# A two-layer encoder in float32 pairs: the first four projection groups ordered by chunk, their weights split at another time

## The chip, the cores and the metric

The kernel runs on one core of one Trainium2 chip. The metric is the device time of one execution in microseconds, lower is better. The core has a matrix engine (PE, with its weight loads PEld), a vector engine (DVE), an activation engine (ACT), GpSimd (POOL) and a sync engine (SP) that here only issues transfers; 16 DMA engines move the data. Each engine works through its own instructions in order and waits on semaphores for the others.

## The reference, cut to what matters

Two groups of 256 tokens (512 in all) go through two encoder layers of width 1024. The part of a layer that the change touches is its start:

```python
def encoder_layer(x, c, ...):                       # called for layer 0 and layer 1
    mod = jax.nn.silu(c) @ w_ada + b_ada            # 6 x 1024 numbers for each group of tokens
    shift1, scale1, gate1, shift2, scale2, gate2 = jnp.split(mod, 6, axis=-1)
    h = rms_norm(x, norm_attn) * (1 + scale1) + shift1
    proj = h @ w_in                                 # qa 512, ka 128, va 128, qb 512, kb 512, vb 512, gates 2048
    ...                                             # two attentions, merge, output projection
    x = x + gate1 * merged
    h2 = rms_norm(x, norm_ffn) * (1 + scale2) + shift2
    return x + gate2 * grouped_moe(h2, ...)         # 16 experts, 2 for each token
```

All of it is float32. The output is the final norm of both groups.

## The kernel before, in words

**Products of pairs.** A float32 product is made of three fast ones. An operand is split into a high part (a copy rounded to the fast type, `x_hi`, `w_hi`) and a low part (the float32 value minus the high part, `x_lo`, `w_lo`). `mm3` (L756) then issues three matmuls of 128x128 by 128x512 into the same bank: low weight by high activation (L758), high weight by low activation (L759), high by high (L760). ACT makes the high parts, DVE the low ones.

**The projection.** The activations are kept transposed, 1024 features as KC = 8 chunks of 128 partitions by 512 tokens. The input projection is cut into groups of 128 output columns (`W_GROUPS`); group n needs a 1024x128 slice of the weight, of which the high part goes into one of W_BUFS = 4 buffers (`w_hi[n % 4]`) and the low part into `w_lo`. `in_group` (L762) takes a bank, waits for the weight's low part and runs eight steps k = 0 to 7, one `mm3` for each chunk: 24 matmuls. Groups 0 to 3 are the four slices of qa, in one 2 MB weight block that lies in ring slot 1; groups 4 and 5 are ka and va. The order of the groups is the list `QKV_ORDER`. In group 0 alone, PE waits before each step for that chunk's low part (`first=True`).

**The chunks.** For chunk c, `norm_scale` (DVE, L1716) multiplies x by the reciprocal root of its mean square. `norm_split` (ACT, L1276) adds shift and scale and rounds to `x_hi`: one pair of instructions for chunks 0 and 4 (`SCALE_DVE`), a pair and a cast for the other six. `norm_low` (DVE, L1727) makes `x_lo`. PE can run step k of any group once chunk k has its low part and the group has its weights.

**The weights of the first four groups.** `high_part(layer, n)` (ACT, L1259) waits for the block to land if n is the block's first group, and casts the slice. `low_part(n)` (DVE, L1709) subtracts. Before, ACT does all four high parts ahead of the first chunk, in both layers; DVE does low part 0 ahead of the first chunk, and low parts 1 to 3 between chunks.

**What stands ahead of it.** In layer 0 the factors `rstd` are known early, and the projection waits for `mod` (from w_ada) and for the block qa. In layer 1 the outputs of the experts are added first: ACT weighs the returned rows (`weigh_first`, L1269), DVE adds the second choice and, chunk by chunk, the result to x (`combine`, L1792, and `add_gated`, L1783). ACT squares each chunk (L1253), PE sums the squares over the partitions (L844), ACT takes the root (`norm_root`, L1255), DVE the reciprocal (L1780). Only then come the chunks.

**What stands behind it.** When a qa group is complete, ACT reads its bank twice (L1361, L1364) and then makes the high part of the group four places later (`GROUP_AFTER`), DVE its low part. PE goes on to group 4 and the rest.

Of the kernel before, what the change touches and what calls it, by code (L numbers as in the profile page):

```python
# [31 lines left out]
KC = D // P  # L32
# [69 lines left out]
W_BUFS = 4  # L102
# [88 lines left out]

GROUP_AFTER = {group_key(n - W_BUFS): n for n in range(W_BUFS, QKV_GROUPS)}
# [145 lines left out]
def build_trunk(nc, t_in, y_prompt, y_sample):  # L340
# [7 lines left out]
    with ctx:  # L348
# [394 lines left out]
        def _(pe):  # L743
# [18 lines left out]
            def in_group(key, n, first=False, before=0):  # L762
# [11 lines left out]
                done(layer_use, key, ins)  # L774

            def ada_rows(layer, i):

# [69 lines left out]
            for layer in range(DEPTH):  # L847
# [20 lines left out]


                for q in QKV_ORDER:  # L870
                    last_block = None
# [28 lines left out]
                    else:  # L900
                        n = group_no("kva", ("ka", "va").index(q)) if q in ("ka", "va") else group_no(q[:2], int(q[2:]))
                        in_group(q, n, first=(n == 0))
                        b = W_GROUPS[n][0]
# [292 lines left out]
        def _(act):  # L1196
# [78 lines left out]

            def norm_split():  # L1276

                for c in range(KC):
                    act.wait_ge(S["xn_ready"], c + 1)
# [31 lines left out]
            for layer in range(DEPTH):  # L1311
# [16 lines left out]
                else:  # L1328
                    for i in range(ADA_FIRST):
                        ada_copy(i)  # L1330
                    weigh_first(layer)
                    for c in range(KC):
                        norm_square(use, "back", c, hT)
                    norm_root(use, 0)
                for n in range(W_BUFS):
                    high_part(layer, n)
                act.wait_ge(S["mod_ready"], 1)
                norm_split()

# [295 lines left out]
        def _(dve):  # L1635
# [156 lines left out]
            def combine(own, use, layer, nth):  # L1792

                for t in range(TT):
                    dve.wait_ge(S["got_weighed"], nth * TT + t + 1)
                    v.scalar_tensor_tensor(got[0][:, t, :], got[1][:, t, :], gw[:, 1, t:t + 1], got[0][:, t, :],
                                           ALU.mult, ALU.add).then_inc(S["mix_ready"], 1)
                for c in range(KC):
                    add_gated(use, ("back", c), c, 1)

            for layer in range(DEPTH):
# [32 lines left out]
                if layer:  # L1834
                    combine(own, use, layer, 0)
                    norm_rstd(own, use, 0)
                low_part(0)
                for c in range(KC + 2):
                    if c < KC:
                        norm_scale(c)  # L1840
                    if c > 1:
                        norm_low(c - 2)
                    if c in (4, 6, 8):
                        low_part(c // 2 - 1)

# [619 lines left out]
```

## Time and profile before

| | us |
|---|---|
| median of 3 runs (1573.08 to 1576.23) | 1575.25 |
| the profiled execution's own time | 1576.64 |
| its span in the trace | 1574.8 |
| PE busy | 1440.8 (91% of the span) |
| DVE busy | 1005.1 (64%) |
| ACT busy | 872.2 (55%) |
| POOL busy | 109.5 (7%) |

Busy time counts all stages together. PE is busy for most of the span, but a matmul lasts longer when the clock granted to PE is low, and that counts as busy too. The two places of the change, the start of the projection of layer 0 and of layer 1, lie at about 43 to 82 us and 793 to 850 us of the trace. What decides there is read from the timelines of the three engines, which tell for each instruction when it began and what ended the idle time before it.

### The profile page before, as it was taken

How to read it: one execution, taken by the hardware profiler on the slowest of the kernel's cores; microseconds unless marked ns; L12 is line 12 of the kernel's file. 1: busy time of each engine (PE TensorE's matmuls, PEld its weight loads, DVE VectorE, ACT ScalarE, POOL GpSimd, SP SyncE). 2: the span in 40 equal slices, each digit the busy share in tenths (PEclk: the TensorE clock that was granted, in tenths of full speed). 3: DMA queues.
4: the chain of work that ended last, by engine and by line, in shares of the span. 5: the costliest groups of instructions: out<-in, count | busy, mean ns of one | idle time of the engine just before them, and what ended most of it. 6: DMA issues, size and time to landing. Idle time of an engine off the chain costs nothing. (4 is left out here: it accounts for less than half of the span.)

```text
span 1574.8 us, 19442 instructions
## 1 busy us (share of the span) xinstructions
PE 1440.8 (91%) x6858; PEld 1095.0 (70%) x6858; DVE 1005.1 (64%) x1256; ACT 872.2 (55%) x1244; POOL 109.5 (7%) x143
## 2 busy tenths in 40 slices
PE   5799999999988999999769989899998899999996
PEld 3477667787757777777437775688875777777774
DVE  1456586334379888888363928743355888888884
ACT  4532486323256777777363318932234577777764
POOL 1000000000011111211000000000000111111100
PEclk9799999999989999999889999999998999999998
DMA  9532471223158999999762217511135599999944
GB/s 328 210 107 107 161 249 73 76 85 107 57 215 310 373 370 354 361 355 361 270 243 85 76 68 267 201 54 54 54 137 184 215 347 366 358 370 358 359 185 164
DMA packets 148368, 341.49 MB, mean 217 GB/s; under 512 B 8351, under 2 KB 10545, under 8 KB 148176
## 3 DMA queue, kind: packets, MB, share of 16 engines
q1 hardware_dynamic: 136880, 317.20, 55.4%
q0 software_dynamic: 10704, 22.57, 4.0%
q10 hardware_dynamic: 720, 0.87, 0.2%
q8 instruction: 39, 0.64, 0.2%
q14 instruction: 25, 0.20, 0.0%
HBM read 333.08 MB, written 24.12 MB: 227 GB/s over the span
## 5 line engine op out<-in xcount | busy, mean ns | idle before, releaser
L758 PE MATMUL bank<-x_hi,w_lo 128*128 128x512 f32 x608 | 246.6, 406 | 28.8 <-DVE x_lo L1736 18.7
L759 PE MATMUL bank<-x_lo,w_hi 128*128 128x512 f32 x608 | 240.0, 395 | 0.0
L760 PE MATMUL bank<-x_hi,w_hi 128*128 128x512 f32 x608 | 240.0, 395 | 0.0
L2217 DVE TENSOR_TENSOR w_lo<-ring,x_lo 128x2048 fp32r<-128x2048 f32 x92 | 210.6, 2289 | 29.5 <-ACT x_lo L1529 28.6
L1529 ACT CAST zone_r<-ring 128x2048 fp32r<-128x2048 f32 x92 | 176.0, 1913 | 28.9 <-PE bank L1106 16.4
L1529 ACT CAST x_lo<-ring 128x2048 fp32r<-128x2048 f32 x92 | 176.0, 1918 | 26.4 <-PE bank L1121 13.6
L1713 DVE TENSOR_TENSOR w_lo<-ring,w_hi 128x1024 fp32r<-128x1024 f32 x84 | 102.4, 1221 | 96.4 <-ACT w_hi L1267 95.7
L758 PEld LDWEIGHTS bank<-x_hi,w_lo 128*128 128x128 f32 x608 | 115.4, 190 | 65.9 <-issue 27.5
L1104 PE MATMUL bank<-w_lo,zone_r 128*128 128x512 f32 x384 | 156.3, 407 | 0.0
L759 PEld LDWEIGHTS bank<-x_lo,w_hi 128*128 128x128 f32 x608 | 116.1, 191 | 25.8 <-issue 2.4
L760 PEld LDWEIGHTS bank<-x_hi,w_hi 128*128 128x128 f32 x608 | 115.8, 190 | 25.0
L1106 PE MATMUL bank<-zone_r 128*128 128x512 f32 x256 | 101.3, 396 | 0.0
L1105 PE MATMUL bank<-zone_r 128*128 128x512 f32 x256 | 100.9, 394 | 0.0
L1267 ACT CAST w_hi<-ring 128x1024 fp32r<-128x1024 f32 x84 | 87.1, 1046 | 20.7 <-PE bank L760 6.1
L1105 PE MATMUL bank<-x_lo,zone_r 128*128 128x512 f32 x240 | 95.1, 396 | 0.0
L1106 PE MATMUL bank<-x_lo,zone_r 128*128 128x512 f32 x240 | 95.0, 396 | 0.0
L1464 ACT ACTIVATE zone<-bank 128x512 f32<-128x512 f32 x32 | 19.1, 598 | 136.1 <-PE bank L760 136.1
L2217 DVE TENSOR_TENSOR w_lo<-ring,zone_r 128x2048 fp32r<-128x2048 f32 x32 | 73.4, 2292 | 21.6 <-ACT zone_r L1529 21.2
L1104 PEld LDWEIGHTS bank<-w_lo,zone_r 128*128 128x128 f32 x384 | 72.4, 189 | 15.3
L2217 DVE TENSOR_TENSOR w_hi<-ring,zone_r 128x2048 fp32r<-128x2048 f32 x32 | 73.4, 2292 | 6.2 <-ACT zone_r L1529 6.0
L2032 DVE TENSOR_TENSOR zone<-bank,zone 128x512 f32<-128x512 f32 x16 | 11.1, 692 | 86.6 <-PE bank L760 86.6
L2217 DVE TENSOR_TENSOR x_hi<-ring,zone_r 128x2048 fp32r<-128x2048 f32 x28 | 63.9, 2283 | 0.0
(316 smaller groups left out, 2751.3 us busy)
## 6 DMA issues: line engine op xcount, KB each, us to landing
ring<-in_w_gate SPq DMA_DIRECT2D x32, 2048.0 KB, 13.8
ring<-in_w_up SPq DMA_DIRECT2D x32, 2048.0 KB, 15.0
ring<-in_w_down SPq DMA_DIRECT2D x32, 2048.0 KB, 9.2
ring<-in_w_ada SPq DMA_DIRECT2D x24, 2048.0 KB, 8.6
ring<-in_w_in SPq DMA_DIRECT2D x16, 2048.0 KB, 8.3
ring<-in_w_out SPq DMA_DIRECT2D x4, 2048.0 KB, 7.7
zone<-y_by_choice SPq DMA_DIRECT2D x8, 1024.0 KB, 8.1
ring<-in_w_branch_a SPq DMA_DIRECT2D x2, 2048.0 KB, 8.0
```

The costliest lines, as they stand in the source:

```text
L758: mm(out, lo, x_first, start=start, stop=False)
L759: mm(out, hi, x_second, start=False, stop=False)
L760: return mm(out, hi, x_first, start=False, stop=stop)
L1104: mm(out, xg_hi[:, par, c, :], wv[:, c, :], start=(c == 0), stop=False)
L1105: mm(out, xg_lo[:, par, c, :], hi[:, k, :], start=False, stop=False)
L1106: ins = mm(out, xg_hi[:, par, c, :], hi[:, k, :], start=False, stop=(c == KC - 1))
L1267: nc.scalar.copy(w_hi[:, n % W_BUFS, :, :], group_view(ring[SLOT[b]], b, c)).then_inc(S["w_hi_ready"], 1)
L1464: af(gates[:, n % 2, :], ps[:, :], ACT.Sigmoid).then_inc(S["gate_ready"], 1)
L1529: nc.scalar.copy(part_hi[buf], ring[EXPERT_SLOTS[par][k]][:, h * 2048:(h + 1) * 2048])\
L1713: v.tensor_tensor(group_view(w_lo[SLOT[b]], b, c), group_view(ring[SLOT[b]], b, c), w_hi[:, n % W_BUFS, :, :].bitcast(F32), ALU.subtract). ...
L2032: v.tensor_tensor(dst, ps[:, :], gates[:, n % 2, :], ALU.mult)\
L2217: v.tensor_tensor(w_low[EXPERT_SLOTS[par][k]][:, cols], ring[EXPERT_SLOTS[par][k]][:, cols], part_hi[buf].bitcast(F32), ALU.subtract)\
```

## The change

Three things change, and the arithmetic stays the same: the same matmuls, casts and subtractions on the same operands.

- PE runs groups 0 to 3 by a list of (group, step) pairs, `FIRST_GROUPS`, and no longer one group after another. It takes groups 0 and 1 for chunks 0 to 3, then groups 2 and 3 for chunks 0 to 3, then all four for chunk 4, then each group's last three steps. Each group has its own bank throughout.
- In layer 0, ACT no longer makes the four high parts first, but one behind chunk 1, 1, 2 and 3 (`SPLIT_ORDER`). DVE's order is `LOW_ORDER` (s: `norm_scale`, x: `norm_low`, w: `low_part`).
- In layer 1, ACT makes the four high parts behind `weigh_first` and ahead of the squares; DVE makes low part 0 ahead of `add_gated`, and low parts 1 to 3 behind it, ahead of the reciprocal.

```diff
+FIRST_GROUPS = ([(n, k) for n in (0, 1) for k in (0, 1)] + [(n, k) for k in (2, 3) for n in (0, 1)]
+                + [(n, k) for n in (2, 3) for k in range(4)] + [(n, 4) for n in range(W_BUFS)]
+                + [(n, k) for n in range(W_BUFS) for k in range(5, KC)])
+SPLIT_ORDER = ("x0", "x1", "w0", "w1", "x2", "w2", "x3", "w3", "x4", "x5", "x6", "x7")
+LOW_ORDER = ("s0", "s1", "x0", "s2", "x1", "w0", "s3", "w1", "x2", "w2", "s4", "x3", "w3", "s5", "x4", "s6", "x5", "s7",
+             "x6", "x7")
...
+            def first_groups():
+                for n, k in FIRST_GROUPS:
+                    b, c = W_GROUPS[n]
+                    if k == 0:
+                        take(layer_use, f"{b}{c}")
+                        pe.wait_ge(S["w_lo_ready"], n + 1)
+                    if n % 2 == 0:
+                        pe.wait_ge(S["x_lo_ready"], k + 1)
+                    ps = bank[layer_use[f"{b}{c}"][0]]
+                    ins = mm3(ps[:, :], w_hi[:, n, k, :], group_view(w_lo[SLOT[b]], b, c)[:, k, :], x_hi[:, k, :],
+                              x_lo[:, k, :], k == 0, k == KC - 1)
+                    if k == KC - 1:
+                        done(layer_use, f"{b}{c}", ins)
...
+                first_groups()
                 for q in QKV_ORDER:
...
-                        in_group(q, n, first=(n == 0))
+                        if n >= W_BUFS:
+                            in_group(q, n)
...
-            def norm_split():
-                for c in range(KC):
+            def norm_split(layer):
+                for what in SPLIT_ORDER:
+                    c = int(what[1:])
+                    if what[0] == "w":
+                        if layer == 0:
+                            high_part(layer, c)
+                        continue
                     act.wait_ge(S["xn_ready"], c + 1)
...
                     weigh_first(layer)
+                    for n in range(W_BUFS):
+                        high_part(layer, n)
                     for c in range(KC):
                         norm_square(use, "back", c, hT)
                     norm_root(use, 0)
-                for n in range(W_BUFS):
-                    high_part(layer, n)
                 act.wait_ge(S["mod_ready"], 1)
-                norm_split()
+                norm_split(layer)
...
+                low_part(0)
                 for c in range(KC):
                     add_gated(use, ("back", c), c, 1)
+                for n in range(1, W_BUFS):
+                    low_part(n)
...
-                low_part(0)
-                for c in range(KC + 2):
-                    if c < KC:
+                for what in LOW_ORDER:
+                    c = int(what[1:])
+                    if what[0] == "s":
                         norm_scale(c)
-                    if c > 1:
-                        norm_low(c - 2)
-                    if c in (4, 6, 8):
-                        low_part(c // 2 - 1)
+                    elif what[0] == "x":
+                        norm_low(c)
+                    elif layer == 0:
+                        low_part(c)
```

PE, start of the projection in layer 0, in the order of issue with bank and buffer numbers. Before, group 0 fills bank 0 and each of its steps waits for a chunk:

```order
L758 MATMUL bank0<-x_hi,w_lo1 128x512 [waits x_lo_ready,w_lo_ready,free0]
L759 MATMUL bank0<-x_lo,w_hi 128x512
L760 MATMUL bank0<-x_hi,w_hi 128x512
L758 MATMUL bank0<-x_hi,w_lo1 128x512 [waits x_lo_ready]
...
L758 MATMUL bank1<-x_hi,w_lo1 128x512 [waits w_lo_ready,free1]
```

In the change (`mm3` stands at L767 to L769), group 1 begins behind step 1 of group 0:

```order
L767 MATMUL bank0<-x_hi,w_lo1 128x512 [waits x_lo_ready,w_lo_ready,free0]
L768 MATMUL bank0<-x_lo,w_hi 128x512
L769 MATMUL bank0<-x_hi,w_hi 128x512
L767 MATMUL bank0<-x_hi,w_lo1 128x512 [waits x_lo_ready]
...
L767 MATMUL bank1<-x_hi,w_lo1 128x512 [waits w_lo_ready,free1]
...
L767 MATMUL bank0<-x_hi,w_lo1 128x512 [waits x_lo_ready]
...
L767 MATMUL bank2<-x_hi,w_lo1 128x512 [waits x_lo_ready,w_lo_ready,free2]
```

The steps of group 0 that wait for chunks 2 and later now stand behind steps of other groups; 32 steps of three matmuls each are issued before and after.

ACT, start of the projection in layer 0. Before, the casts of the block qa stand first and wait for its landing:

```order
L1267 CAST w_hi<-ring 128x1024 [waits ada_rows,landed1]
L1267 CAST w_hi<-ring 128x1024 x3
L1284 ACTIVATE x_hi<-hT,mod 128x256 [waits xn_ready,mod_ready]
L1284 ACTIVATE x_hi<-hT,mod 128x256
L1286 ACTIVATE hT<-hT,mod,mul 128x256 [waits xn_ready]
```

In the change, the chunks 0 and 1 stand ahead of that wait:

```order
L1315 ACTIVATE x_hi<-hT,mod 128x256 [waits ada_rows,xn_ready,mod_ready]
L1315 ACTIVATE x_hi<-hT,mod 128x256
L1317 ACTIVATE hT<-hT,mod,mul 128x256 [waits xn_ready]
L1317 ACTIVATE hT<-hT,mod,mul 128x256
L1321 CAST x_hi<-hT 128x512 [waits h_ready_a]
L1293 CAST w_hi<-ring 128x1024 [waits landed1]
L1293 CAST w_hi<-ring 128x1024
```

Two of the four casts stand behind chunk 1, and one each behind chunks 2 and 3.

DVE, start of layer 1. Before, the four low parts stand behind the reciprocal:

```order
L1796 SCALAR_TENSOR_TENSOR zone<-zone,gw 128x1024 [waits got_weighed] x3
L1788 SCALAR_TENSOR_TENSOR xT<-bank,mod,xT 128x256 [waits full0]
...
L1780 RECIPROCAL rstd<-root 128x512 [waits free2]
L1713 TENSOR_TENSOR w_lo<-ring,w_hi 128x8x128 [waits w_hi_ready,dve_own]
```

In the change, one stands ahead of the first addition to x and three ahead of the reciprocal:

```order
L1827 SCALAR_TENSOR_TENSOR zone<-zone,gw 128x1024 [waits got_weighed] x3
L1744 TENSOR_TENSOR w_lo<-ring,w_hi 128x8x128 [waits w_hi_ready]
L1819 SCALAR_TENSOR_TENSOR xT<-bank,mod,xT 128x256 [waits full0]
...
L1744 TENSOR_TENSOR w_lo<-ring,w_hi 128x8x128 [waits w_hi_ready] x3
L1811 RECIPROCAL rstd<-root 128x512 [waits free2]
```

The additions to x now stand behind a wait for ACT's first cast of the block qa, and so behind the landing of that block.

## Rows read from the trace of the kernel before

**Rows 1.** The page: busy time, and the clock granted to PE in 40 slices

```profile
PE 1440.8 (91%) x6858; PEld 1095.0 (70%) x6858; DVE 1005.1 (64%) x1256; ACT 872.2 (55%) x1244; POOL 109.5 (7%) x143
...
PEclk9799999999989999999889999999998999999998
```

**Rows 2.** Timeline of PE, layer 0: start, duration, operation, idle time before and releaser

```profile
52.71 0.77 PE L758 MATMUL bank<-x_hi,w_lo 128*128 128x512 f32 x1 [9.98 <-DVE x_lo L1736]
...
63.23 0.63 PE L758 MATMUL bank<-x_hi,w_lo 128*128 128x512 f32 x1
...
64.51 0.63 PE L758 MATMUL bank<-x_hi,w_lo 128*128 128x512 f32 x1
...
69.61 0.39 PE L758 MATMUL bank<-x_hi,w_lo 128*128 128x512 f32 x1
...
70.29 0.39 PE L758 MATMUL bank<-x_hi,w_lo 128*128 128x512 f32 x1
...
82.28 0.47 PE L758 MATMUL bank<-x_hi,w_lo 128*128 128x512 f32 x1 [0.26 <-issue]
```

**Rows 3.** Two stretches of layer 0: length, busy time by engine, granted clock, DMA

```profile
52.70:60.00 7.30, 6.60 (x13) 3.80 (x14) 6.98 (x12) 7.16 (x14) 0.00 (x0) 0.50 1.04 374
65.00:70.00 5.00, 5.00 (x23) 4.16 (x22) 1.23 (x1) 2.23 (x3) 0.00 (x0) 0.98 0.00 0
```

**Rows 4.** Timeline of ACT, layer 0

```profile
46.96 3.88 ACT L1267 CAST w_hi<-ring 128x1024 fp32r<-128x1024 f32 x4 [5.00 <-DMA ring<-in_w_in]
...
50.75 0.90 ACT L1284 ACTIVATE x_hi<-hT,mod 128x256 fp32r<-128x256 f32 x2
...
51.56 1.08 ACT L1286 ACTIVATE hT<-hT,mod,mul 128x256 f32<-128x256 f32 x2
...
53.19 1.09 ACT L1286 ACTIVATE hT<-hT,mod,mul 128x256 f32<-128x256 f32 x2
...
65.72 0.60 ACT L1361 ACTIVATE zone<-bank 128x512 f32<-128x512 f32 x1 [2.82 <-PE bank L760]
```

**Rows 5.** Timeline of DVE, layer 0

```profile
43.32 0.17 DVE L1771 SCALAR_TENSOR_TENSOR mul<-mod,cur 128x16 f32<-128x16 f32 x1
...
48.03 1.23 DVE L1713 TENSOR_TENSOR w_lo<-ring,w_hi 128x1024 fp32r<-128x1024 f32 x1 [4.54 <-ACT w_hi L1267]
...
51.68 0.88 DVE L1736 SCALAR_TENSOR_TENSOR x_lo<-hT,mod,x_hi 128x256 fp32r<-128x256 f32 x2 [0.43 <-ACT x_hi L1284]
...
68.28 1.23 DVE L1713 TENSOR_TENSOR w_lo<-ring,w_hi 128x1024 fp32r<-128x1024 f32 x1 [4.21 <-ACT w_hi L1267]
```

**Rows 6.** Timeline of PE, layer 1

```profile
819.98 0.77 PE L758 MATMUL bank<-x_hi,w_lo 128*128 128x512 f32 x1 [8.30 <-DVE x_lo L1736]
...
822.90 0.51 PE L758 MATMUL bank<-x_hi,w_lo 128*128 128x512 f32 x1
...
849.76 0.47 PE L758 MATMUL bank<-x_hi,w_lo 128*128 128x512 f32 x1 [0.26 <-issue]
```

**Rows 7.** Timeline of ACT, layer 1

```profile
793.49 4.27 ACT L1273 ACTIVATE zone<-zone,gw 128x1024 f32<-128x1024 f32 x4
...
811.72 0.69 ACT L1257 ACTIVATE root<-bank,eps 128x512 f32<-128x512 f32 x1 [1.35 <-PE bank L844]
...
812.30 3.87 ACT L1267 CAST w_hi<-ring 128x1024 fp32r<-128x1024 f32 x4
```

**Rows 8.** Timeline of DVE, layer 1

```profile
802.05 6.36 DVE L1788 SCALAR_TENSOR_TENSOR xT<-bank,mod,xT 128x256 f32<-128x256 f32 x16 [2.10 <-PE bank L835]
...
812.44 3.35 DVE L1780 RECIPROCAL rstd<-root 128x512 f32<-128x512 f32 x1 [4.03 <-ACT root L1257]
```

**Rows 9.** The load of the block qa in layer 1, and its landing

```profile
L653 SPq DMA_DIRECT2D ring<-in_w_in x1: 382/382/382, 785.5 to 785.5; - x1
...
DMA to landing us min/median/max: 14.8/14.8/14.8
```

**Rows 10.** A stretch of an expert's down projection, PE alone

```profile
508.86:513.98 5.12, 5.12 (x24) 1.00 1.05 390
```

## The prediction

> **What bounds the kernel now.** I read the page first: PE is busy for 91% of the span, and its granted clock falls below full in a few places only, among them the start of each layer [rows 1]. So most of the span is PE at work, and what can be had there is little; the change works where PE waits. The second view is PE's timeline at the start of layer 0 [rows 2]: PE stood idle for 9.98 us until 52.71, ended by the low part of chunk 0. The first matmul of group 4 began at 82.28 after 0.26 us of idle, so groups 0 to 3 ended at 82.0. Between, two paces: a step of three matmuls took 1.28 us (63.23 to 64.51) and later 0.68 us (69.61 to 70.29). The windows give the reason: granted clock 0.50 (1.2 GHz) in 52.7 to 60, nearly full (2.4 GHz) from 65 on [rows 3]. PE was also held back by the chunks: busy for 6.60 of 7.30 us at the low clock. The third view are the timelines of ACT and DVE [rows 4, 5]. ACT waited 5.00 us for the block qa and cast it for 3.88 us; only then came chunk 0 at 50.75, then a chunk each 1.63 us (51.56 to 53.19; chunks 0 and 4 take 0.81). DVE stood 4.54 us in its first low part, although what the chunks need was there at 43.5 [rows 5]. Layer 1 is alike: PE starts at 819.98, group 4 at 849.76 [rows 6], and the four casts and low part 0 stand behind the root [rows 7, 8].
>
> **A formula for this stretch.** Groups 0 to 3 are 32 steps. If PE never waits inside them, they end at start + 32 x 0.68 + 0.47 x (time at the low clock), since each us at 1.28 a step instead of 0.68 loses 1 - 0.68/1.28 = 0.47 us; that is start + 21.8 + 0.47 x low. Layer 0 before: 52.7 + 21.8 + 0.47 x 12.2 (until about 64.9) = 80.2, and the real end is 82.0: 1.8 us were waits for chunks. Layer 1 before ended at 849.5.
>
> **Part 1, layer 0, the start.** No instruction is added; order alone changes. The chunks may begin at 43.5. DVE scales chunk 0 (0.87, as a pair of this kind takes) until 44.4; ACT does chunk 0 until 45.3 and chunk 1 until 46.9. That is the time at which the block lands (ACT's wait ended at 46.96 [rows 4]), so the wait goes, and its cover is the two chunks; the load itself isn't moved on SP's queue. Cast 0 then ends at 48.0, DVE's low part 0 (1.23) at 49.3, and PE starts at 49.45, with the 0.15 us that stood between DVE's end (51.68 + 0.88) and 52.71 [rows 2, 5]. Gain at the start: 3.25 us.
>
> **Part 2, layer 0, the 32 steps.** ACT's whole work here is 6 x 1.63 + 2 x 0.81 + 3.88 = 15.3 us; from 44.5 that is 59.8, with waits for DVE about 61.3, and chunk 7's low part is there at 62.0. Step 23 in the list is the first to need chunk 7, and PE gets there at about 67. Low part 1 is there at 51.1 and needed at 52.0; chunk 2 at 51.6, needed at 54.6; chunk 3 at 54.3, needed at 56. So PE has no wait, the nearest by 0.9 us. What remains is the clock. PE's idle time before is still nearly 7 us, so it starts low. How long it stays so, the trace doesn't show for this order; the rows bound it: 2.9 us in layer 1 (the matmul of 822.90 is the first that lasts 0.51 instead of 0.63) and 12.2 us in layer 0. I take 5 us: near the layer 1 row, since PE now has work without gaps, and some more since chance decides when it rises. End: 49.45 + 21.8 + 2.35 = 73.6 against 82.0, a gain of **8.4 us** (9.4 with 2.9 us, 5.0 with 12.2).
>
> **Part 3, layer 0, the end.** The four banks now fill within 6.1 us: group 0 is complete nine steps (9 x 0.68) ahead of group 4, not 16. Before, ACT began on group 0's bank at 65.72, and low part 4 ended at 68.28 + 1.23 = 69.5 [rows 4, 5]: 3.8 us. That fits in 6.1; groups 5, 6 and 7 need ACT 2.6 us each against PE's 5.45 a group. Cost nothing, as long as ACT is through with chunk 7 (61.3 against 67.5, the end of group 0).
>
> **Part 4, layer 1, ahead of the root.** ACT ends its weighing at 793.49 + 4.27 = 797.8 and has nothing until DVE's additions (802.05 [rows 7, 8]). The block lands at 785.5 + 14.8 = 800.3 [rows 9]. Casts: 800.3 to 804.2. Low part 0 on DVE: 801.4 to 802.6, so the additions begin 0.55 us late and end at 808.95. ACT's first square moves from 803.0 to 804.2, but PE's sums wait for the bank of chunk 2, which comes with the additions; so the root, and the reciprocal behind it, come 0.55 late: 816.35 in place of 815.8. Low parts 1 to 3 take 3.5 us, until 812.5, and the root comes at 811.72 + 0.69 + 0.55 = 812.95: hidden, by 0.4 us only. Behind the reciprocal, low part 0 (1.2 us) is gone, and chunk 0's low part no longer stands behind another chunk. PE starts at 816.35 + 0.87 + 0.9 + 0.88 + 0.25 for the handovers = 819.25, against 819.98: 0.75 us.
>
> **Part 5, layer 1, the 32 steps.** ACT gives a chunk each 1.63 us, so chunk 1 is there at 820.6 (0.1 to 0.2 us of wait), chunk 3 at 823.8, chunk 7 at 830.1; PE at 1.28 and then 0.68 a step needs them at 820.5, 825, 837. With 4.5 us at the low clock (2.9 is the row, and again 12.2 the far end): 819.25 + 0.2 + 21.8 + 2.1 = 843.35 against 849.5, a gain of **6.15 us** (6.9 and 2.5 at the ends).
>
> **Sum.** 8.4 + 6.15 = 14.5 us. Profiled execution: 1576.64 - 14.5 = 1562.1; it stands 1.4 us above the median, so against the median of 1575.25 I forecast **1560.8 us**, 0.92% less. From group 4 on, everything waits for PE or follows it, so I let the gain pass through. With the ends of the clock alone: 1559.0 to 1567.8.
>
> **The rivals.**
> 1. *As computed*, clock up after 3 to 7 us: 1559 to 1563. For it: every wait named in rows 2, 4, 5 and 6 is one of order. Chance 0.76.
> 2. *The low clock stays*, some 12 us in each layer, since PE gets small waits at semaphores after all: 5.0 + 2.5 = 7.5, time 1567.7. For it: it did so in layer 0. Against: there 1.8 us of waits lay in between. Chance 0.08.
> 3. *Layer 1 waits for its block.* The landing at 800.3 is already 0.55 us too late to be hidden: each us later puts DVE's additions, and all behind them, 1 us later, which before had 12 us to spare. 6 us late, and layer 1's gain is gone: 1566.9. Against: the loads ahead of it are the same. Chance 0.05.
> 4. *Absorbed later*: a transfer that comes at its own time stops PE, and the time stays near 1575. Against: PE's wait ahead of group 4 was 0.26 us of issue. Chance 0.04.
> 5. *More*: the clock rises almost at once: 10.7 + 8.2 = 18.9, time 1556.3. Chance 0.04.
> 6. *Slower*: steps that change from bank to bank keep PE at the low clock. Then 32 x 1.28 = 41 us a layer: ends at 90.4 and 860.5, 8.4 and 11.0 later than before, time 1594.7. It decides where the low clock lasts over 23 us (49.45 + 21.8 + 0.47 x 23 = 82). Against it: the down projection of an expert changes banks after each three matmuls in the same way, and 24 matmuls took 5.12 us at clock 1.00 [rows 10], no slower than the 0.68 us of a step here. Chance 0.03. The Trainium skill (TensorE: Matmul & The Clock Gate, section "A second HAM failure mode: psum-queue depth-cycling") says that a kernel which cycled through its banks left PE with small idle times between matmul groups, and the clock went up and down. By that rule this rival would be the likely one; the rows of the down projection speak against it here.
>
> **How the numbers follow.** The time is that of case 1. The range runs from case 5 to the ends of cases 2 and 3: **1556.3 to 1568.0**. Outside are cases 4 and 6. About 0.2% (3.2 us) can be told from no change. Cases 1, 2, 3 and 5 are faster: 0.93. Case 4 is the same, 0.04, and case 6 slower, 0.03.
>
> **What would show it.** PE's first projection matmul 3.2 us earlier in layer 0 and 0.5 to 1 us in layer 1; no wait for `x_lo` behind the first steps; group 4 at about 74 us and, from there to the weighing of the rows in layer 1, all 8 to 9 us earlier; in layer 1 the additions 0.5 us later behind the weighing, group 4 then 50 us behind the weighing (56.3 before, 849.76 - 793.49). The prediction is wrong if DVE waits in layer 1 for ACT's cast by more than 2 us, if PE waits at group 4 for `w_lo`, or if the clock is at half for over 7 us.

## The result, and the profile after

The changed kernel took **1565.87 us** (median of 4 runs, 1562.28 to 1567.48); the kernel before, on the same chip, 1575.74 us (4 runs, 1573.08 to 1577.4). The ratio is 0.9936, with a 95% interval of 0.992 to 0.9952: 9.9 us faster by the medians. The forecast was 14.5 us, so the sign is right and the time lies in the range, but a third of the gain is missing, and the time lies above the 1559 to 1563 us of case 1. The profiled execution took 1566.96 us. Here and below, times are medians and a ratio compares means, so a ratio is not exactly the quotient of the two medians beside it.

The page has PE busy for 3.8 us less than before. Of the 40 slices of the granted clock two differ by a tenth from those of before [rows 1]: the second (39 to 78 us, with the start of layer 0) rose from 7 to 8, and the 21st (783 to 822 us, with the start of layer 1) fell from 8 to 7.

```profile
span 1565.1 us, 19441 instructions
...
PE 1437.0 (92%) x6858; PEld 1093.7 (70%) x6858; DVE 1006.0 (64%) x1256; ACT 871.6 (56%) x1244; POOL 109.4 (7%) x143
...
PEclk9899999999989999999879999999998999999998
```

PE's timeline at the start of layer 0 (start, duration, operation, idle time before and its releaser) answers to [rows 2]: first matmul at 50.41, group 4 at 74.48 in place of 82.28.

```profile
50.41 0.76 PE L767 MATMUL bank<-x_hi,w_lo 128*128 128x512 f32 x1 [6.77 <-DVE w_lo L1744]
...
74.48 0.47 PE L767 MATMUL bank<-x_hi,w_lo 128*128 128x512 f32 x1 [0.26 <-DVE w_lo L1744]
```

The windows (length, then busy time of PE, PEld, DVE, ACT and POOL, granted clock, DMA share, GB/s) of the 32 steps in both layers. PE is busy without a gap, and the low clock (0.50, that is 1.2 GHz) lasts for 3.6 us in layer 0 and 5.4 us in layer 1, against 12.2 us in layer 0 in this profile of before (some 5 us in its second profile, see the last experiment):

```profile
50.40:54.00 3.60, 3.59 (x9) 2.83 (x10) 3.60 (x5) 3.54 (x7) 0.00 (x0) 0.50 1.04 364
54.00:74.20 20.20, 20.20 (x89) 16.41 (x87) 9.56 (x14) 12.38 (x21) 0.00 (x0) 1.00 0.38 139
813.30:818.70 5.40, 5.35 (x12) 3.97 (x13) 4.72 (x9) 4.77 (x10) 0.00 (x0) 0.50 0.00 0
818.70:837.90 19.20, 19.20 (x85) 15.62 (x83) 6.33 (x9) 10.28 (x17) 0.00 (x0) 1.00 0.00 1
```

ACT and then DVE in layer 0, beside [rows 4, 5]. ACT's chunks 0 and 1 stand ahead of the casts, which no longer wait for the block; the bank of group 0 is read at 68.14, and DVE ends low part 4 at 70.69 + 1.22 = 71.9, 2.6 us ahead of group 4.

```profile
45.57 0.91 ACT L1315 ACTIVATE x_hi<-hT,mod 128x256 fp32r<-128x256 f32 x2 [2.69 <-DVE hT L1754]
...
48.02 1.99 ACT L1293 CAST w_hi<-ring 128x1024 fp32r<-128x1024 f32 x2
...
68.14 0.60 ACT L1392 ACTIVATE zone<-bank 128x512 f32<-128x512 f32 x1 [6.00 <-PE bank L769]
...
69.60 1.05 ACT L1293 CAST w_hi<-ring 128x1024 fp32r<-128x1024 f32 x1 [0.29 <-ACT zone L1395]
```

```profile
44.25 0.17 DVE L1802 SCALAR_TENSOR_TENSOR mul<-mod,cur 128x16 f32<-128x16 f32 x1
...
49.09 1.23 DVE L1744 TENSOR_TENSOR w_lo<-ring,w_hi 128x1024 fp32r<-128x1024 f32 x1 [0.25 <-ACT w_hi L1293]
...
70.69 1.22 DVE L1744 TENSOR_TENSOR w_lo<-ring,w_hi 128x1024 fp32r<-128x1024 f32 x1 [7.82 <-ACT w_hi L1293]
```

PE in layer 1, beside [rows 6]: the transposes of the returned rows (L859), the sums of squares (L868), the first projection matmul, and group 4.

```profile
788.72 5.04 PE L859 MATMUL bank<-const,zone 128*128 128x128 f32 x32 [2.27 <-DVE zone L1827]
797.43 8.83 PE L868 MATMUL bank<-hT,const 128*128 128x512 f32 x16 [3.67 <-DVE xT L1819]
813.35 0.76 PE L767 MATMUL bank<-x_hi,w_lo 128*128 128x512 f32 x1 [7.09 <-DVE x_lo L1767]
...
838.25 0.47 PE L767 MATMUL bank<-x_hi,w_lo 128*128 128x512 f32 x1 [0.29 <-DVE w_lo L1744]
```

The first two of these rows in the kernel before were:

```profile
796.41 6.64 PE L835 MATMUL bank<-const,zone 128*128 128x128 f32 x32 [2.27 <-DVE zone L1796]
804.54 7.13 PE L844 MATMUL bank<-hT,const 128*128 128x512 f32 x16 [1.49 <-DVE xT L1788]
```

ACT and DVE in layer 1, beside [rows 7, 8]:

```profile
785.79 4.27 ACT L1299 ACTIVATE zone<-zone,gw 128x1024 f32<-128x1024 f32 x4
792.72 3.88 ACT L1293 CAST w_hi<-ring 128x1024 fp32r<-128x1024 f32 x4 [2.65 <-DMA ring<-in_w_in]
796.51 2.31 ACT L1279 ACTIVATE hT<-xT 128x512 f32<-128x512 f32 x4
...
806.30 0.69 ACT L1283 ACTIVATE root<-bank,eps 128x512 f32<-128x512 f32 x1 [3.04 <-PE bank L868]
```

```profile
793.79 1.23 DVE L1744 TENSOR_TENSOR w_lo<-ring,w_hi 128x1024 fp32r<-128x1024 f32 x1 [1.54 <-ACT w_hi L1293]
794.94 6.35 DVE L1819 SCALAR_TENSOR_TENSOR xT<-bank,mod,xT 128x256 f32<-128x256 f32 x16
...
807.02 3.35 DVE L1811 RECIPROCAL rstd<-root 128x512 f32<-128x512 f32 x1 [2.33 <-ACT root L1283]
```

Since layer 1 is reached 7.7 us earlier, its times are best read from the start of ACT's weighing (793.49 before, 785.79 after):

| behind the weighing, us | before | forecast | after |
|---|---|---|---|
| DVE's additions to x begin | 8.56 | 9.1 | 9.15 |
| PE's sums begin (and last) | 11.05 (7.13) | 11.6 (7.1) | 11.64 (8.83) |
| reciprocal begins | 18.95 | 19.5 | 21.23 |
| first projection matmul | 26.49 | 25.75 | 27.56 |
| group 4 begins | 56.27 | 49.9 | 52.46 |

Up to the start of the sums all goes as forecast. **The sums then last 1.7 us longer**, and from there on layer 1 is late. What they lost is clock. In the columns above, first the stretch from the transposes to the sums in the kernel after, then the first 2.6 us of the sums and the rest of them: the clock is at 1.00, then 0.67 and 0.86.

```profile
791.50:797.40 5.90, 2.26 (x21) 2.02 (x19) 4.36 (x9) 4.68 (x6) 0.00 (x0) 1.00 1.07 373
797.40:800.00 2.60, 2.57 (x4) 1.16 (x5) 2.60 (x7) 2.27 (x5) 0.00 (x0) 0.67 1.05 388
800.00:806.30 6.30, 6.26 (x13) 2.39 (x11) 4.69 (x7) 2.93 (x5) 0.00 (x0) 0.86 0.73 270
```

In the kernel before, the end of the transposes with the wait behind it, and then the whole of the sums, at clock 1.00:

```profile
799.00:804.50 5.50, 4.06 (x22) 3.82 (x20) 3.40 (x8) 1.26 (x2) 0.00 (x0) 0.69 1.07 370
804.50:811.70 7.20, 7.13 (x16) 2.96 (x16) 3.90 (x10) 5.06 (x7) 0.00 (x0) 1.00 1.05 387
```

The ledger of the profiled executions, before minus after (1576.64 - 1566.96 = 9.7): group 4 of layer 0 begins 7.8 us earlier (forecast 8.4); at the weighing it is 7.7; layer 1 adds 3.8 (forecast 6.15), which makes 11.5 at its group 4; and between there and the end 1.8 us are given back. So of the missing 4.8 us, 0.6 and 2.3 belong to places of the change, and some 2 to stages that the change doesn't touch.

### The profile page after: what moved, and what is told of

Its sections match the earlier page's. It is cut to its first block and busy times, and to the rows that moved or that the text cites. A ratio compares the mean times of both kernels' runs of the same rounds, so it can differ in the third digit from the quotient of the medians.

```text
span 1565.1 us, 19441 instructions
## 1 busy us (share of the span) xinstructions
PE 1437.0 (92%) x6858; PEld 1093.7 (70%) x6858; DVE 1006.0 (64%) x1256; ACT 871.6 (56%) x1244; POOL 109.4 (7%) x143
## 5 line engine op out<-in xcount | busy, mean ns | idle before, releaser
L767 PE MATMUL bank<-x_hi,w_lo 128*128 128x512 f32 x608 | 244.0, 401 | 19.7 <-DVE w_lo L1744 7.3
L769 PE MATMUL bank<-x_hi,w_hi 128*128 128x512 f32 x608 | 238.7, 393 | 0.0
L767 PEld LDWEIGHTS bank<-x_hi,w_lo 128*128 128x128 f32 x608 | 115.3, 190 | 51.6 <-issue 23.0
L769 PEld LDWEIGHTS bank<-x_hi,w_hi 128*128 128x128 f32 x608 | 115.1, 189 | 24.5
```

The costliest lines, as they stand in the source:

```text
L767: mm(out, lo, x_first, start=start, stop=False)
L769: return mm(out, hi, x_first, start=False, stop=stop)
```

## The experiments

Four questions: which part of the change earns the gain; why the sums take longer; what the low clock at the two starts costs; and whether the stages behind lose time because of the change. Each run's profile is read by the milestones of the table above.

### The change once more

> The change itself, again, for a closer measurement beside the other three. Both theories: about 10 us below the kernel before. If the clock of the matrix engine falls at other points in this execution, the stages of it differ by 1 to 2 us from the first profile: the sums over the partitions at the start of layer 1 take 7.1 us where the clock is full and 8.8 where it isn't.

Measured: 1566.46 us (6 runs, 1561.97 to 1566.85) against 1574.04; ratio 0.9944 (0.9927 to 0.9962). Group 4 of layer 0 began at 74.08, the sums lasted 8.83 us again, group 4 of layer 1 came 52.23 us behind the weighing. The slow sums belong to the kernel, not to one execution. But this execution lost time at another place: the weighing began at 787.04, only 6.45 us earlier than before, because the last 7 us of layer 0's attention ran at a low clock. The same stretch in the two executions of the same program, first this one, then the one above:

```profile
235.00:242.00 7.00, 6.22 (x29) 4.51 (x29) 3.62 (x4) 5.57 (x12) 0.00 (x0) 0.56 0.50 200
```

```profile
235.00:242.00 7.00, 5.45 (x36) 4.24 (x37) 3.46 (x4) 6.43 (x17) 0.00 (x0) 1.00 0.57 233
```

From the last projection matmul to the merge it took 76.8 us here and 74.7 us there. That is a scatter of 2 us that no order in the code decides.

### PE's order alone

`first_groups` in the kernel before, with ACT's and DVE's orders as before:

```diff
+                first_groups()
...
-                        in_group(q, n, first=(n == 0))
+                        if n >= W_BUFS:
+                            in_group(q, n)
```

> Only the order of the first four groups on PE is changed; ACT and DVE are as before. Theory (the steps of other groups fill the waits for chunks): the first matmul stays where it was in both layers, the low clock ends after 4 to 6 us, and with about 1.5 us of wait for low part 1 groups 0 to 3 end 2.7 us earlier in layer 0 and 3.9 us in layer 1: 6.5 us below the kernel before. Rival (what counts is when chunks and weights are there): under 2 us.

Measured: 1567.90 us (12 runs, 1563.56 to 1574.16) against 1574.04; ratio 0.9961 (0.9945 to 0.9978): 6.1 us, most of the gain. PE's timeline, layer 0 and layer 1:

```profile
51.90 0.77 PE L762 MATMUL bank<-x_hi,w_lo 128*128 128x512 f32 x1 [8.68 <-DVE x_lo L1757]
...
78.76 0.47 PE L762 MATMUL bank<-x_hi,w_lo 128*128 128x512 f32 x1 [0.26 <-DVE w_lo L1734]
```

```profile
800.89 7.13 PE L863 MATMUL bank<-hT,const 128*128 128x512 f32 x16 [1.77 <-DVE xT L1809]
...
843.22 0.47 PE L762 MATMUL bank<-x_hi,w_lo 128*128 128x512 f32 x1 [0.26 <-DVE w_lo L1734]
```

Layer 0 starts at 51.90, where the casts stand first, and reaches group 4 after 26.9 us (before 29.6, the change 24.1): it waits 1.23 us for low part 1 and has 7.8 us of low clock. Layer 1 reaches group 4 at 52.27 us behind the weighing (790.95), as soon as the whole change does. Its sums lasted 7.13 us. Not all of this is the work of the order: in layer 1, 1.1 of the 4.0 us came ahead of the first projection matmul, with transposes of 5.25 us in place of 6.64, and in layer 0, 0.8 of the 3.5 us was an earlier start, which the kernel before shows too in its second profile (52.05). The 32 steps themselves took 2.7 and 2.9 us less.

### ACT's and DVE's orders alone

The change with groups 0 to 3 run one after another again:

```diff
-                first_groups()
...
-                        if n >= W_BUFS:
-                            in_group(q, n)
+                        in_group(q, n, first=(n == 0))
```

> Only ACT's and DVE's orders are changed, in both layers; PE runs group after group as before. Theory: group 0 still follows the chunks one by one to the last, which comes 1.9 us earlier in layer 0 and 0.8 us later (behind the weighing) in layer 1: about 1 us below the kernel before, between 0 and 3. Rival (the split of the orders carries the gain): 5 us or more.

Measured: 1575.44 us (12 runs, 1573.41 to 1578.44) against 1574.04; ratio 1.0009 (0.9999 to 1.0019). No gain. PE's timeline in layer 0:

```profile
49.09 0.77 PE L767 MATMUL bank<-x_hi,w_lo 128*128 128x512 f32 x1 [6.77 <-DVE w_lo L1742]
...
53.98 0.79 PE L767 MATMUL bank<-x_hi,w_lo 128*128 128x512 f32 x1 [0.71 <-DVE x_lo L1760]
...
56.58 0.80 PE L767 MATMUL bank<-x_hi,w_lo 128*128 128x512 f32 x1 [0.95 <-DVE x_lo L1765]
...
79.23 0.47 PE L767 MATMUL bank<-x_hi,w_lo 128*128 128x512 f32 x1 [0.26 <-issue]
```

PE starts as early as in the change, but group 0 now runs at the pace of the chunks, which have the casts between them: it waits for the low parts at 53.98 and 56.58 (and less at later steps), keeps the low clock until 61.6, and reaches group 4 30.1 us after its start. In layer 1 the sums lasted 8.83 us and group 4 came 56.42 us behind the weighing, against 56.27 before. The profile still shows 3 us less in layer 0 (1.9 us against the second profile of before), and the median 1.4 us more than before; where the runs lost the rest I can't say, since one execution only has a trace. What holds is that the early start alone gave nothing. With PE's order the two parts together gave 7.6 us here, more than the 4.7 that 6.1 and -1.4 add up to; since the intervals of the change and of PE's order alone are some 2.7 us wide to each side, this difference is not shown.

### Low part 0 behind the additions

Is it DVE's low part 0 ahead of the additions that holds the sums up?

```diff
-                low_part(0)
                 for c in range(KC):
                     add_gated(use, ("back", c), c, 1)
-                for n in range(1, W_BUFS):
+                for n in range(W_BUFS):
                     low_part(n)
```

> The change, but in layer 1 low part 0 stands behind the additions to x, with the other three, and no longer ahead of them. Theory (the delayed additions leave PE idle for 3.7 us, the clock falls, and the sums over the partitions take 8.8 us in place of 7.1): additions start 8.6 us behind the first weighing and not 9.2, PE's idle time ahead of the sums is under 3.2 us, the sums take about 7.1 us; the reciprocal waits about 0.3 us for the low parts; 1.5 to 2 us below the change. Rival (the clock falls there by chance of the moment, in either order): the same as the change within 1 us, and sums of 7 to 9 us in both.

Measured: 1565.91 us (6 runs, 1562.67 to 1567.84) against 1574.04; ratio 0.9945 (0.9928 to 0.9962): as the change. The additions began 6.88 us behind the weighing in place of 9.24 in the change's profile on this chip, and still the sums came no earlier and lasted 8.80 us. PE's row, then ACT's:

```profile
798.44 8.80 PE L868 MATMUL bank<-hT,const 128*128 128x512 f32 x16 [4.22 <-ACT hT L1279]
```

```profile
793.88 3.88 ACT L1293 CAST w_hi<-ring 128x1024 fp32r<-128x1024 f32 x4 [3.00 <-DMA ring<-in_w_in]
797.67 4.26 ACT L1279 ACTIVATE hT<-xT 128x512 f32<-128x512 f32 x8
```

PE's releaser is now ACT's square. ACT's four casts stand ahead of the squares, and wait for the block; they end at 797.8. So two things hold the sums at the same time, low part 0 on DVE and the four casts on ACT, and taking away one shows nothing. That DVE's alone did it, is wrong.

### Layer 1 as before

PE's order and layer 0 as in the change; in layer 1 the casts behind the root and, by the loop of before that the diff leaves out, the low parts between the chunks:

```diff
                     weigh_first(layer)
-                    for n in range(W_BUFS):
-                        high_part(layer, n)
                     for c in range(KC):
                         norm_square(use, "back", c, hT)
                     norm_root(use, 0)
+                    for n in range(W_BUFS):
+                        high_part(layer, n)
...
-                low_part(0)
                 for c in range(KC):
                     add_gated(use, ("back", c), c, 1)
-                for n in range(1, W_BUFS):
-                    low_part(n)
```

> The change, but in layer 1 the high and low parts of the four weights stand where they stood before (behind the root, low parts between the chunks). Theory (what moving them ahead gives behind the reciprocal it takes away ahead of it, since PE is idle for 3.7 us and more ahead of the sums and these then take 8.8 us): additions 7.4 to 8.6 us behind the first weighing, sums 7.1 us, group 4 in layer 1 at 52 us behind the weighing, the time within 1.5 us of the change. Rival (the weights ahead of the root carry a part of the gain): 2 to 4 us above the change.

Measured: 1564.92 us (5 runs, 1562.59 to 1565.55) against 1574.16; ratio 0.9932 (0.992 to 0.9945). **The part of the change in layer 1 shows no gain**; without it the median is no higher. PE's timeline, with the weighing at 785.05:

```profile
794.42 7.13 PE L868 MATMUL bank<-hT,const 128*128 128x512 f32 x16 [1.77 <-DVE xT L1819]
...
836.60 0.47 PE L767 MATMUL bank<-x_hi,w_lo 128*128 128x512 f32 x1 [0.26 <-DVE w_lo L1744]
```

The sums wait 1.77 us and last 7.13. PE's first projection matmul comes 24.81 us behind the weighing (27.56 in the change), the 32 steps take 26.7 us (24.9). The early weights save 1.8 us in the steps and cost 2.75 ahead of them.

### Half of the casts ahead of the squares

If the four casts and low part 0 are too much ahead of the sums, two casts might do: ACT makes high parts 0 and 1 ahead of the squares and 2 and 3 behind them, DVE low parts 0 to 2 behind the additions and the last one between the chunks.

```diff
-                    for n in range(W_BUFS):
+                    for n in (0, 1):
                         high_part(layer, n)
                     for c in range(KC):
                         norm_square(use, "back", c, hT)
+                    for n in (2, 3):
+                        high_part(layer, n)
...
-                low_part(0)
                 for c in range(KC):
                     add_gated(use, ("back", c), c, 1)
-                for n in range(1, W_BUFS):
+                for n in range(3):
                     low_part(n)
...
-                    elif layer == 0:
+                    elif layer == 0 or c == 3:
                         low_part(c)
```

> The change, but in layer 1 ACT makes two of the four high parts ahead of the squares and two behind them, and DVE makes low parts 0 to 2 behind the additions and low part 3 between the chunks. Theory (the wait ahead of the sums is what costs): idle of PE ahead of the sums 1.5 to 1.8 us, sums 7.1 us, PE's first matmul 25.5 us behind the weighing and not 27.6, group 4 at 50 us and not 52.3; 2 us below the change. Rival (the clock falls ahead of the sums in any case): sums of 8.8 us, and the time within 1 us of the change.

Measured: 1564.66 us (6 runs, 1558.74 to 1567.83) against 1574.16; ratio 0.9934 (0.9914 to 0.9954). The median is 1.2 and 1.8 us below those of the change, which were taken on other chips; this is inside the spread of the runs. The mechanism is plain in the profile, PE first and then ACT (the weighing at 786.28):

```profile
796.24 7.10 PE L868 MATMUL bank<-hT,const 128*128 128x512 f32 x16 [2.27 <-ACT hT L1279]
810.52 0.77 PE L767 MATMUL bank<-x_hi,w_lo 128*128 128x512 f32 x1 [7.18 <-DVE x_lo L1769]
...
835.14 0.47 PE L767 MATMUL bank<-x_hi,w_lo 128*128 128x512 f32 x1 [0.26 <-DVE w_lo L1746]
```

```profile
793.57 1.99 ACT L1293 CAST w_hi<-ring 128x1024 fp32r<-128x1024 f32 x2 [3.02 <-DMA ring<-in_w_in]
795.47 3.23 ACT L1279 ACTIVATE hT<-xT 128x512 f32<-128x512 f32 x6
...
800.17 1.98 ACT L1293 CAST w_hi<-ring 128x1024 fp32r<-128x1024 f32 x2
```

PE stands idle for 2.27 us, the sums last 7.10, and group 4 comes 48.86 us behind the weighing, 3.6 us earlier than in the change. The four casts are now 2 x 1.99 us on both sides of the squares, and hidden on both.

> halves again, for a closer time and a second profile. Theory: group 4 in layer 1 at 49 to 50 us behind the weighing again; executions in two groups, some 4 us apart, by the clock at the end of attention and in the experts; 0 to 2 us below the change. Rival: the first profile was a lucky one, group 4 at 52 us.

Once more on a third chip, beside the kernel below: 1564.63 us (6 runs, 1563.44 to 1566.81) against 1574.34; ratio 0.9942 (0.9928 to 0.9957). The idle time was 1.77 us, the sums 7.13, group 4 at 49.32. So the profile holds, twice, but the times don't show it: the ratios 0.9934 and 0.9942 are those of the change (0.9936 and 0.9944) and of the kernel with layer 1 as before (0.9932). That the halves are faster as a whole is not shown.

### PE kept busy ahead of the first step

What is the low clock at the two starts worth? Matmuls that nobody reads, ahead of the first groups, on operands that are there; they take PE's idle time and nothing else:

```diff
+            def busy_ahead(layer):
+                b, n = layer_use[("back", KC - 1) if layer else ("ada_cols", ADA_FIRST - 1)]
+                pe.wait_ge(free[b], n + 1)
+                for _ in range((6, 7)[layer]):
+                    mm(bank[b][:, :], K("ones"), const[:, 0:512], start=True, stop=True)
...
+                busy_ahead(layer)
                 first_groups()
```

> The change, with matmuls added that nobody reads: ahead of the first group, into bank 7 once that is free, six of 128x128 by 128x512 in layer 0 and seven in layer 1, so that PE isn't idle there. Theory (the formula, 0.47 us for each us at the low clock): low clock in the 32 steps from 3.6 and 5.3 us to under 1, each stretch 22 us long; 3 to 4 us below the change. Rival (the clock isn't kept up by these, or the steps wait for chunks as soon as they are faster): less than 1.5 us below it.

Measured: 1566.03 us (6 runs, 1561.6 to 1568.21) against 1574.16; ratio 0.9937 (0.9923 to 0.9952). The windows of the 32 steps (96 matmuls) in layers 0 and 1:

```profile
50.20:73.30 23.10, 22.63 (x96) 17.76 (x96) 13.18 (x18) 16.01 (x28) 0.00 (x0) 1.00 0.48 172
815.20:838.20 23.00, 22.33 (x96) 17.87 (x96) 11.11 (x17) 15.16 (x27) 0.00 (x0) 1.00 0.00 1
```

The clock is full from the first step, and groups 0 to 3 take 23.2 and 23.0 us in place of 24.1 and 24.9: 2.8 us. The median shows none of it. Its profile lost 2.1 us at the end of layer 0's attention, where the change's first profile did not, and the runs spread over 6.6 us; so this run alone doesn't decide.

> Both together: halves and busy. Theory: the two add up, 5 to 6 us below the change, about 1560, unless the chunks, one each 1.63 us from ACT, begin to hold PE up in layer 1, which would take back up to 1 us. Rival: no better than the better of the two.

With both edits: 1561.50 us (5 runs, 1560.38 to 1565.26) against 1574.16; ratio 0.9913 (0.99 to 0.9926). Group 4 of layer 0 at 73.99, of layer 1 48.76 us behind the weighing, beside 48.86 in the kernel with halves alone, so the unread matmuls add nothing there. The clock was full at the first step, but PE had waited 1.30 us ahead of it and 0.42 us for the second chunk, and the eight matmuls from 813.77 to 816.83 lasted 0.63 us again, as at the low clock. In layer 0 the 32 steps took 23.1 us against 24.8. The end of the attention was at the low clock in this execution too. The median is 3.2 us below that of halves, of which 1.7 have this place; the two ranges overlap.

### The end of the attention as well

One such matmul behind each of two of the last turns of the attention, where PE has small gaps and the clock fell in some profiles:

```diff
                         for slot in range(3):
                             turn(p - 1, slot)
+                            if p == PERIODS and slot < 2:
+                                b, n = layer_use[("scores_b", PERIODS - 1, 0)]
+                                pe.wait_ge(free[b], n + 1)
+                                mm(bank[b][:, :], K("ones"), const[:, 0:512], start=True, stop=True)
```

> busy_halves with two more matmuls that nobody reads in each layer, between the three turns of the last period of attention, where PE waits 1.2 and 0.8 us. Theory (the idle times there let the clock fall in some executions, which costs 2.2 us each time): no low clock at the end of attention in either layer, that stage at 74.7 us in both, executions within 3 us of each other, and 1 to 2 us below busy_halves. Rival (that stretch comes whatever PE does there, or the added matmuls delay the turns by what they save): the same as busy_halves within 0.7 us.

Measured: 1560.40 us (6 runs, 1558.77 to 1562.86) against 1574.34; ratio 0.9914 (0.99 to 0.9929). From the last projection matmul to the merge it took 74.7 us in both layers, and this kernel's runs spread over 4.1 us. It is 13.9 us below before and 4.2 below the kernel with halves on the same chip, two ranges that don't meet. But the kernel with halves and unread matmuls had the same ratio without these two, and seven of the twelve other profiles, those of the kernel before among them, have 74.6 to 74.9 us in both layers without them; so what they add by themselves is not shown.

### The kernel before once more

> The kernel before, unchanged, for a second profile of it. Theory (a part of the forecast gain is lost where the clock falls in some executions at the end of attention, in the kernel before too): its stage from the last projection matmul to the merge takes 74.7 us, or 76.8 with the low clock in its last 7 us. Rival (the kernel before never has that): 74.7 us, and nothing else differs from the first profile by over 0.5 us.

Measured: 1572.72 us in one execution; the 11 other runs of the kernel before on this chip gave 1571.33 to 1577.04, median 1574.34. From the last projection matmul to the merge it took 74.6 us in both layers, so neither profile of this kernel shows the low clock there. Layer 1 answers to the first trace almost row by row: the transposes ahead of the additions 6.63 us (6.64), the sums 7.13, group 4 of layer 1 56.24 us behind the weighing. In layer 0 group 4 came 1.2 us earlier and the weighing 1.3, and the clock took another course: the last matmul at the low clock began at 56.06, 4 us behind the start, and not 12 us behind it.

```profile
56.06 0.63 PE L760 MATMUL bank<-x_hi,w_hi 128*128 128x512 f32 x1
57.38 0.50 PE L758 MATMUL bank<-x_hi,w_lo 128*128 128x512 f32 x1 [0.69 <-DVE x_lo L1731]
```

Yet groups 0 to 3 took 29.05 us here and 29.57 there. With some 7 us less of low clock PE waited longer for the chunks instead. By these two profiles the low clock cost little in the old order, and what the new order removes is mainly the pace of the chunks.

The span is 3.9 us shorter than in the first profile, so the stages behind layer 1's group 4 alone differ by 2.6 us between two executions of one program. A giving back of 1.8 us is no larger than that, and I don't ascribe it to the change.

## Why the prediction was right, and where it was not

**Parts 1 and 2 held.** Start at 50.41 (49.45 forecast; 49.09 in the second profile): the factors of `mod` came 0.9 us later in the first (44.25 against 43.32 [rows 5]), and ACT's first chunk with them. The low clock lasted 3.6 us (5.8 in the second profile), forecast 5. The formula gives 50.41 + 21.8 + 0.47 x 3.6 = 73.9 for the end, and group 4 began at 74.48 after 0.26 us of idle. The gain is 7.8 and, in the second profile, 8.2 us, against 8.4; measured from the second profile of before, where group 4 began at 81.10, it is 6.6 and 7.0. PE had no wait among the 32 steps. What the part took for the cost of the kernel before, 12.2 us of low clock and 1.8 us of waits, was one execution's share: with some 5 us of low clock the waits were 4.6 us by the same formula (81.10 - 0.35 - 52.05 - 21.8 - 0.47 x 5), and the total moved by 0.5 only.

**Part 3 held.** Four banks filling together cost nothing: low part 4 was ready 2.6 us ahead of its use. One figure of it was wrong: before, group 0 was complete 24 steps, or 16 us, ahead of group 4, not 16 steps.

**Part 4 failed**, at one sentence: "PE's sums wait for the bank of chunk 2 ... so the root, and the reciprocal behind it, come 0.55 late". The 0.55 was right (0.59) and the sums began as forecast. I carried their duration over unchanged, 7.1 us; it was 8.83. The reason is PE's idle time ahead of them. It was 1.49 us before and 3.67 after. The thirteen profiles fall in two sorts with nothing between:

| kernels | idle ahead of the sums, us | sums, us |
|---|---|---|
| before (twice), PE's order alone, layer 1 as before, halves (twice), halves with unread matmuls (twice) | 1.49 to 2.27 | 7.10 to 7.13 |
| the change (twice), ACT's and DVE's orders alone, low part 0 behind, unread matmuls alone | 3.67 to 4.29 | 8.80 to 8.83 |

The Trainium skill (TensorE: Matmul & The Clock Gate, section "HAM oscillation — how this bites in real kernels") says that a long wait of PE brings it back to the low rate, so that the work behind the wait starts slow. By that rule a wait of PE costs twice, itself and what follows at half the rate; the trace agrees in the cost, with 1.7 us behind an idle time that grew by 2.2, though the clock fell only 0.9 us into the sums.

Why did the idle time grow by 2.2 us when the additions came only 0.59 later? Because PE had its work ahead of it done sooner: the transposes (L835 before, L859 after) took 6.64 us in the kernel before and 5.04 after. Before, most of them ran at the low clock (0.50 until 802), and the additions waited for them; 8.56 us behind the weighing was what PE's low clock set, and 6.88 is what the additions need (layer 1 as before, transposes 4.68 us). The block's landing and low part 0 put them at 9.15. So my delay of 0.55 us was measured against a start that was itself late; against the earliest possible one it was 2.3. One rival remains: in all thirteen profiles the long idle time goes with four casts ahead of the squares. No run makes the wait longer without them, or fills this wait with unread matmuls, so that the idle time itself brings the clock down is the likeliest reading and not a proof. Rival 3, which had the block's landing as its mechanism, named the right place with a chance of 0.05 and counted only a later landing.

**Part 5 held** for what it treats: 813.35 + 21.8 + 0.47 x 5.4 = 837.7 against 838.0. The gain of the steps came, 4.9 us of 5.4; 0.75 us of gain at the start was a loss of 1.07. Layer 1: 3.8 us in place of 6.15. The 2.9 us that I took from the kernel before as its low clock in layer 1 were only the first stretch of it: in the same trace the matmuls from 829.80 to 832.34 last 0.63 us again. Of the three signs of being wrong none came: DVE waited 1.54 us for ACT's cast, PE's 0.29 us ahead of group 4 was no longer than before, and the low clock lasted 3.6 and 5.4 us.

**The sum** also let the gain pass through to the end without loss. It did so to the weighing (7.8 to 7.7). Behind layer 1's group 4 1.8 us went, which two executions of the kernel before differ by as well. Medians of six runs carry 1 to 2 us of chance here. So the range was met, but not by the ways that set its upper end: the low clock was short, the block landed when it should, and the time came out between case 1 and case 2 for reasons that no case names. That it lies inside is in part luck.

**Rivals.** The low clock didn't stay (rival 2), nor rise at once (5). Rival 6 is refuted by the window 54.0 to 74.2: clock 1.00 and 0.68 us a step, although the bank changes 15 times among the 32 steps (3 times before). The Trainium skill's rule on cycling through the banks (TensorE: Matmul & The Clock Gate, section "A second HAM failure mode: psum-queue depth-cycling") isn't seen at work here; in the kernel with unread matmuls ahead, all 32 steps ran at full clock.

## What to carry to other kernels

Moving work ahead of a wait is free only while nothing that PE waits for stands behind it on the same engine: here casts ahead of the squares and a subtraction ahead of the additions cost 2.75 us to save 1.8 in the profile, and two casts and no subtraction cost nothing there. Read the slack of an engine from the earliest time its inputs could be there, not from when it last happened to start, since the start shown may itself be set by a low clock. And price a longer idle time of PE with what the matmuls behind it then take, not with its own length alone.

## What was not expected of the hardware

- The same 16 matmuls of the sums took 7.1 us behind 1.5 to 2.3 us of idle and 8.8 us behind 3.7 to 4.3, in all thirteen profiles; in the changed kernel the clock was still 1.00 over 791.5 to 797.4, through the whole wait, and fell at about 798.3, 0.9 us into the sums.
- The last 7 us of layer 0's attention ran at a mean clock of 1.00 in one execution and of 0.56 in another of the same program, which cost 2.1 us. It came in five of the thirteen profiles, in four at layer 0 and in one at layer 1. What decides it is open.
- The transposes of the returned rows took 6.64 and 6.63 us in the two profiles of the kernel before, 5.04 to 5.25 in three others and 4.68 in eight, with the same instructions there. The longer ones ran in part at the low clock; what set how much, stays open.
- In the kernel before, the first four groups of layer 0 took 29.6 us with 12.2 us of low clock and 29.05 with some 5: a low clock costs little while PE would wait for its operands anyway.
